# Weight loads in 4 KB rows, column groups for a two-column product, and gathers issued ahead of their stage, in a two-block transformer kernel

## Chip, cores and metric

The kernel runs on one core of one Trainium2 chip. The metric is the device time of one execution in microseconds (us), the median of the runs taken. One launch computes everything.

## What is computed

Two blocks of two layers each (`DEPTH = 2`) over 256 tokens of width 1024, float32 throughout. The second block also carries 256 context tokens of its own.

```python
def first_block(x, ...):
    for l in range(DEPTH):
        h = rms_norm(x, attn_norm_g[l])
        pa, pb, pc = split_sizes(h @ w_in[l], (A_PROJ, B_PROJ, C_PROJ))
        ya = rwkv7_mixer(pa, ...); yb = dilated_mixer(pb, ...); yc = mla_mixer(pc, ...)
        x = x + jnp.concatenate([ya, yb, yc], axis=-1) @ w_out[l]
        h = rms_norm(x, ffn_norm_g[l])
        x = x + (jax.nn.silu(h @ ffn_w_gate[l]) * (h @ ffn_w_up[l])) @ ffn_w_down[l]

def second_block(x, c, ctx, c_ctx, ada_w, ada_b, ...):
    for i in range(DEPTH):
        mod = jax.nn.silu(c) @ ada_w[i] + ada_b[i]          # one row of 6 * 1024
        modc = jax.nn.silu(c_ctx) @ ada_w[i] + ada_b[i]     # and one for the context
        ...                                                 # modulated norms, attention, projection
        x = x + g2 * peer_ffn(h2, ...)
        if not last:
            xc = xc + cg2 * peer_ffn(h2c, ...)

def peer_block(hb, w_q, sub_keys, u_tab, v_tab):
    ...                                    # 8 heads x 16 experts for each token
    u = u_tab[expert]                      # gathered rows of 1024 floats
    act = jax.nn.gelu(jnp.einsum('nhkd,nd->nhk', u, hb))
    w = g * act
    return jnp.einsum('nhk,nhkd->nd', w, v_tab[expert])
```

## The kernel before

The program is a sequence of stages (`stage`, L151). In each the five engines run their own streams, kept in order by semaphores, and each ends in a block end and a barrier (L157 to L161): an engine drains its own work, and all wait for the last. The order is: the modulation of the second block's first layer; qkv, attention and projection of the context tokens; their expert queries (the choice of 128 expert slots per token, `SLOTS`); then the first block, two layers of in_projection, rwkv, latent_heads, first_attention, out_projection and feed_forward; then the second block's latent tokens: qkv, attention, out projection, peer_queries, experts, twice.

**Weights.** `WeightRing` (L164) has three slots in SBUF (`WSLOTS`). A group of weights is one image [128, n] in HBM, mostly n = 4096 floats for 8 k-tiles by 512 columns: 16 KB per partition, 2 MB, loaded by one `dma_start` of SyncE (`load_to`, L175). Before loading over slot g - 3, SyncE waits until `w_used` says that TensorE is through with it. For that TensorE, after the last product of each group, waits for its own product semaphore and then adds one to `w_used` (L411 for the in projection; such a pair stands behind each group in every stage). A layer of the first block has 5 groups for in_projection, 6 of the modulation weights of the second block's second layer (used inside rwkv), 1 for the latent queries, 1 for the latent keys and values, 2 for out_projection, 11 for gate and up, 6 for down.

**Modulation.** [silu(c), silu(c_ctx)] are two columns. For each of 12 groups of 512 output columns (L1499) the stationary operand is silu[:, k, :] (128x2) and the weights [128, 512] move, eight k-tiles into two PSUM partitions; ScalarE copies the two rows out and four transposes (L1509) turn them into columns. In rwkv the same product is done in parts (`mod_part`, L485) between the levels of a triangular inverse, copied by ScalarE to a row buffer and written to HBM (`kept_mod`) by one DMA per group; the second layer's experts stage reads it back and transposes it.

**Context expert rows.** The context tokens' experts are not computed in a stage of their own: `ContextRows` (L1222) spreads 232 gathers per layer of the first block over its stages. A row is one indirect DMA of GpSimd (L1249) that brings one expert's 1024 floats for each of 128 tokens, 4 KB per partition, 512 KB in all, into one of four slots (`CTX_RING`). U rows (slots 0 to 127) are each consumed by one VectorE instruction with a sum (L1261), V rows by one that adds a weighted row to a running sum (L1265). Between them stand the gelu weights (`gelu_weights`), in feed_forward ahead of the first V rows. `SHARE` says how many rows each stage has: in_projection 26, rwkv 70, latent_heads 4, attention 14, out_projection 12, feed_forward 106. `fetch` issues them in the stage that takes them, each waiting until the row four before has been taken; `take(v, n)` stands in VectorE's stream between its other work, three rows per tile in in_projection and feed_forward, and `take_rest` takes what is left at the stage's end. `ContextTail` does the same for 48 last rows in the second block's first layer.

In feed_forward, for each of 22 tiles (`FF_TILES`) TensorE does gate and up (32 products of 256 columns), ScalarE the sigmoid, VectorE the two multiplications (`acted`), with four PSUM banks in turn: TensorE can't start tile j before tile j - 4 is multiplied. Then come the down products, 352 of them.

Of the kernel before, what the change touches and what calls it, by code (L numbers as in the profile page):

```python
# [7 lines left out]
F32 = mybir.dt.float32  # L8
# [44 lines left out]
WSLOT = KT * 544  # L53

# [109 lines left out]
class WeightRing:  # L164
# [10 lines left out]
    def load_to(self, eng, g1):  # L175

        for g in range(self.started, min(g1, len(self.sizes))):
            if g >= WSLOTS:
                eng.wait_ge(self.mem.w_used, g - WSLOTS + 1)
            n, at = self.sizes[g], self.offsets[g]  # L180
            eng.dma_start(self.slot(g)[:, 0:n], self.images[at:at + P * n].rearrange("(p n) -> p n", p=P)
                          ).then_inc(self.mem.w_landed[g % WSLOTS], 16)
        self.started = max(self.started, min(g1, len(self.sizes)))

    def landed(self, eng, g):
        eng.wait_ge(self.mem.w_landed[g % WSLOTS], 16 * (g // WSLOTS + 1))
# [175 lines left out]
def in_projection(nc, m, d, ring, l, rows):  # L362

    with stage(nc, NORM_SEMS + " loras prod_done evacuated mixed step_v h_in",
# [6 lines left out]
        dest = [b.pad[:, j, 1:SEQ + 1] for j in range(A_TILES)]  # L371
# [18 lines left out]
        def _(pe):  # L390
            norm_pe(pe, m, s, b, SEQ)
            for j, (g, c, n) in enumerate(tiles):
# [45 lines left out]
def rwkv(nc, m, d, ring, l, rows):  # L438
# [13 lines left out]
    with stage(nc, sems, bufs) as (block, s, b):  # L452
# [14 lines left out]
        mod_row = lambda n: m.mix[0:2, 2 + 2 * (n % 2):4 + 2 * (n % 2), :].rearrange("p f t -> p (f t)")  # L467

        @block.sync
        def _(sp):  # L470
            for n in range(MODS):
                ring.load_to(sp, g0 + G_MOD + WSLOTS + n + 1)
                sp.wait_ge(s.mod_copied, n + 1)
                sp.dma_start(m.kept_mod[:, 512 * (l * MODS + n):512 * (l * MODS + n + 1)], mod_row(n)).then_inc(
                    mod_kept(n), 16)
            for n in range(2):
                sp.wait_ge(mod_kept(n), 16 * MODS // 2)
# [6 lines left out]
        def _(pe):  # L484
            def mod_part(n, k0, k1):  # L485
# [6 lines left out]
                for k in range(k0, k1):  # L492
                    ins = pe.matmul(m.ps[0:2, mod_bank(n), :], m.silu[:, k, :], w[:, k, :], start=(k == 0),
                                    stop=(k == KT - 1), skip_group_check=True)
                if k1 == KT:
                    ins.then_inc(s.mod_done, 1)
                    pe.wait_ge(s.mod_done, n + 1)
                    pe.sem_inc(m.w_used, 1)
# [16 lines left out]
            mod_part(0, 0, KT)  # L515
# [24 lines left out]
            for lev in range(LEVELS):  # L540
# [12 lines left out]
                mod_part(lev, 0, 2)  # L553
# [7 lines left out]
                mod_part(lev, 2, KT)  # L561
# [1665 lines left out]
```

## Time and profile before

| | us |
|---|---|
| median of 3 runs (3628.1 to 3643.7) | 3635.93 |
| the profiled execution | 3640.52 |
| its span, first to last instruction | 3638.7 |

Over the span TensorE is busy 76%, VectorE 61%, GpSimd 33%, ScalarE 16%, with a mean granted TensorE clock of 0.909. The DMA engines move 1026 MB, 282 GB/s. A shared view of busy times says little here, since the stages have different limits. In the profile's 40 slices the expert stages stand out (DMA 9, some 420 GB/s), and between them stand stretches at 70 GB/s. The stages, from the trace:

| stage | from | to, us |
|---|---|---|
| modulation | 0.8 | 103.8 |
| context qkv, attention, projection, queries | 105 | 365 |
| layer 0: in_projection | 370.4 | 450.6 |
| rwkv | 451.8 | 650.9 |
| latent_heads | 653.5 | 679.8 |
| attention | 681.6 | 727.1 |
| out_projection | 728.2 | 762.3 |
| feed_forward | 762.8 | 1060.4 |
| layer 1, the same six stages | 1062.8 | 1760.5 |
| latent qkv, attention, projection, queries | 1785 | 2032 |
| experts | 2032 | 2697 |
| qkv, attention, projection, queries | 2698 | 2969 |
| experts | 2969 | 3632 |

The names in the rows below: `ps` is PSUM, `w_ring` the weight slots, `ctx_ring` the four row slots, `in_peer_u`, `in_peer_v` the expert tables. SPq, ACTq and POOLq are the queues' issuing instructions; q0 holds the DMA packets of the gathers, q1 those of the weight loads.

### The profile page before, as it was taken

The numbers are of one execution on the slowest core, as the hardware profiler recorded it, in microseconds if no ns is written. First come the engines' busy times: TensorE is split into PE (matmuls) and PEld (weight loads), VectorE is DVE, ScalarE is ACT, GpSimd is POOL, SyncE is SP. The second block draws the span as 40 slices with busy tenths as digits, with TensorE's granted clock in tenths as the row PEclk, the third lists the DMA queues.
The fourth block names the chain that finished last, engine by engine and source line by source line (L and its number), as shares of the span: only waits on it lengthen the run. The fifth ranks groups of instructions, "written<-read, shape, count | busy, mean of one in ns | idle before, by whom it ended". The sixth has DMA issues, their size and how long they took to land. (4 is left out here: it accounts for less than half of the span.)

```text
span 3638.7 us, 31139 instructions
## 1 busy us (share of the span) xinstructions
PE 2775.6 (76%) x10098; PEld 1770.8 (49%) x10098; DVE 2227.2 (61%) x5250; ACT 581.0 (16%) x1595; POOL 1187.8 (33%) x1028
## 2 busy tenths in 40 slices
PE   8893778599937868997489587777779957777776
PEld 1672646478735556786457232232237743233222
DVE  0439576755556757545676787665546377766555
ACT  0311110210002002000131111111112211111111
POOL 0000344234543432445222244444410014444442
PEclk9996988899968969998699799999989989999999
DMA  8322776578868746788455699999961239999997
GB/s 339 129 93 72 266 266 228 168 276 324 325 245 298 276 167 219 296 327 324 150 170 180 267 420 420 421 421 421 420 246 70 71 140 421 420 419 421 421 420 304
DMA packets 166034, 1026.31 MB, mean 282 GB/s; under 512 B 18552, under 2 KB 19544, under 8 KB 86896
## 3 DMA queue, kind: packets, MB, share of 16 engines
q0 software_dynamic: 147456, 805.37, 56.8%
q1 hardware_dynamic: 17552, 214.67, 15.5%
q10 hardware_dynamic: 864, 4.28, 0.3%
q8 instruction: 81, 1.33, 0.1%
q14 instruction: 81, 0.66, 0.1%
HBM read 1020.53 MB, written 3.72 MB: 281 GB/s over the span
## 5 line engine op out<-in xcount | busy, mean ns | idle before, releaser
L2140 PE MATMUL ps<-w_ring,diag 128*128 128x512 f32 x1216 | 577.2, 621 | 173.5 <-ACT diag L2103 173.3
L1249 POOL DMA_INDIRECT ctx_ring<-in_peer_u,ctx_expert x256 | 306.1, 1196 | 871.7 <-POOLq L161 478.2
L2023 DVE SCALAR_TENSOR_TENSOR w_ring<-w_ring,htok 128x1024 f32<-128x1024 f32 x304 | 372.2, 1225 | 237.8 <-DMA w_ring<-in_peer_uv,expert 237.3
L2140 PEld LDWEIGHTS ps<-w_ring,diag 128*128 128x128 f32 x1216 | 227.3, 195 | 519.2 <-ACT diag L2103 279.3
L2140 PE MATMUL ps<-own,diag 128*128 128x512 f32 x624 | 312.5, 643 | 204.1 <-ACT diag L2103 204.1
L2010 POOL DMA_INDIRECT w_ring<-in_peer_uv,expert x304 | 333.4, 1097 | 409.5 <-PE ps L2140 397.4
L1261 DVE SCALAR_TENSOR_TENSOR ctx_ring<-ctx_ring,h_now 128x1024 f32<-128x1024 f32 x256 | 306.7, 1224 | 143.8 <-DMA ctx_ring<-in_peer_u,ctx_expert 135.1
L1249 POOL DMA_INDIRECT ctx_ring<-in_peer_v,ctx_expert x208 | 275.7, 1326 | 297.9 <-DVE sum L1265 120.8
L2010 POOL DMA_INDIRECT own<-in_peer_uv,expert x156 | 164.0, 1051 | 631.3 <-POOLq L161 364.5
L1167 PE MATMUL ps<-mix,w_ring 128*128 128x256 f32 x1408 | 316.8, 387 | 19.0 <-DVE mix L354 8.6
L2140 PEld LDWEIGHTS ps<-own,diag 128*128 128x128 f32 x624 | 117.5, 200 | 392.3 <-ACT diag L2103 277.6
L1167 PEld LDWEIGHTS ps<-mix,w_ring 128*128 128x128 f32 x1408 | 270.9, 194 | 65.0 <-issue 23.8
L2023 DVE SCALAR_TENSOR_TENSOR own<-own,htok 128x1024 f32<-128x1024 f32 x156 | 191.0, 1225 | 136.8 <-DMA own<-in_peer_uv,expert 136.7
L2103 ACT ACTIVATE diag<-consts_sb,w 128x128 f32<-128x128 f32 x512 | 177.5, 394 | 576.5 <-DVE w L2040 576.5
L1265 DVE SCALAR_TENSOR_TENSOR low<-ctx_ring,ctx_weight,low 128x1024 f32<-128x1024 f32 x104 | 133.5, 1283 | 120.5 <-DMA ctx_ring<-in_peer_v,ctx_expert 115.9
L1265 DVE SCALAR_TENSOR_TENSOR sum<-ctx_ring,ctx_weight,sum 128x1024 f32<-128x1024 f32 x104 | 133.5, 1283 | 119.5 <-DMA ctx_ring<-in_peer_v,ctx_expert 114.5
L326 PE MATMUL ps<-sq,consts_sb 128*128 128x256 f32 (+1 forms) x96 | 38.3, 575 | 194.6 <-ACT sq L334 194.6
L1182 PE MATMUL ps<-act,w_ring 128*128 128x256 f32 x704 | 154.8, 380 | 3.7 <-PE ps L1182 2.8
L1182 PEld LDWEIGHTS ps<-act,w_ring 128*128 128x128 f32 x704 | 132.8, 190 | 25.7 <-issue 8.1
L2098 ACT ACTIVATE th<-th 128x2 f32<-128x2 f32 x256 | 52.1, 203 | 525.5 <-DVE th L2032 525.5
L1891 PE MATMUL ps<-hT,w_ring 128*128 128x256 f32 x512 | 121.2, 393 | 9.9 <-issue 5.0
L406 PE MATMUL ps<-mix,w_ring 128*128 128x256 f32 x544 | 122.6, 386 | 7.6 <-DVE mix L354 6.1
(395 smaller groups left out, 4092.2 us busy)
## 6 DMA issues: line engine op xcount, KB each, us to landing
w_ring<-in_weights SPq DMA_DIRECT2D x93, 2048.0 KB, 9.2
w_ring<-in_peer_uv,expert POOLq DMA_INDIRECT x304, 15.8
w_ring<-in_weights SPq DMA_DIRECT2D x2, 2176.0 KB, 10.6
ctx_ring<-in_peer_u,ctx_expert POOLq DMA_INDIRECT x256
w_ring<-in_weights SPq DMA_DIRECT2D x4, 1024.0 KB, 8.0
ctx_ring<-in_peer_v,ctx_expert POOLq DMA_INDIRECT x208
own<-in_peer_uv,expert POOLq DMA_INDIRECT x156, 16.6
consts_sb<-in_consts ACTq DMA_DIRECT2D x1, 1867.0 KB, 17.6
```

The lines of the kernel that those rows point to most:

```text
L406: ins = pe.matmul(m.ps[:, j % BANKS, 0:SEQ], w[:, k, c:c + P], m.hT[:, k, 0:SEQ], start=(k == 0), stop=(k == KT - 1))
L1167: ins = pe.matmul(m.ps[:, GU[j % 4], part * SEQ:(part + 1) * SEQ], w[:, k, (j % 2) * P:(j % 2 + 1) * P], m.hT[:, k, 0:SEQ], start=(k == 0) ...
L1182: ins = pe.matmul(m.ps[:, 2 + o // 2, (o % 2) * SEQ:(o % 2 + 1) * SEQ], w[:, kk, o * P:(o + 1) * P], b.act[:, j, :], start=(j == 0 and o % ...
L1249: pool.indirect_dma_start(out=m.ctx_ring[:, r % CTX_RING, :], out_offset=None, in_=expert_tables(self.d)[r // SLOTS], in_offset=bass.Indir ...
L1261: v.scalar_tensor_tensor(out=row, in0=row, scalar=1.0, in1=m.h_now[:, :], op0=ALU.mult, op1=ALU.mult, accum_out=m.ctx_dots[:, k:k + 1]).th ...
L1265: v.scalar_tensor_tensor(out=m.tail_sum[self.l], in0=row, scalar=m.ctx_weight[:, self.l, k:k + 1], in1=m.tail_sum[self.l], op0=ALU.mult, o ...
L1891: ins = pe.matmul(m.ps[:, j % 4, 0:SEQ], w[:, k, (j % 4) * P:(j % 4 + 1) * P], m.hT[:, k, 0:SEQ], start=(k == 0), stop=(k == KT - 1))
L2010: pool.indirect_dma_start(out=entry(e), out_offset=None, in_=table, in_offset=bass.IndirectOffsetOnAxis(ap=m.expert[:, blk, k:k + 1], axis ...
L2023: v.scalar_tensor_tensor(out=u, in0=u, scalar=1.0, in1=m.htok[:, blk, :], op0=ALU.mult, op1=ALU.mult, accum_out=b.dots[:, e:e + 1]).then_i ...
L2098: act.activation(th, th, ACT.Tanh, scale=math.sqrt(2 / math.pi)).then_inc(s.tanh_out, 1)
L2103: act.activation(b.diag[:, e % DIAGS, :], m.ident, ACT.Copy, scale=b.w[:, e:e + 1]).then_inc(s.built, 1)
L2140: ins = pe.matmul(m.ps[:, 2 * blk + half, :], b.diag[:, e % DIAGS, :], entry(e)[:, D + half * 512:D + (half + 1) * 512], start=(k == 0), s ...
```

## The change

- `load_to` splits each group into pieces of 1024 floats per partition (`PIECE`): four DMAs of 512 KB instead of one of 2 MB, with rows of 4 KB instead of 16 KB. `landed` waits for all of a group's pieces.
- `w_used` is gone. `load_to` gets a function that names, for each group of this stage, the product semaphore and count after which the slot is free; SyncE waits on that. TensorE's wait and increment behind each group go. Groups of earlier stages need no wait, since the barrier has passed.
- The two-column product uses column groups: `silu` gets 32 columns, 30 of them zero, and for each of two steps four matmuls of different k-tiles write four ranges of 32 PSUM partitions. The four partial sums are added afterwards, in modulation by a product with a 128x2 matrix `pick` of ones in place of the transpose, in the experts stage by four accumulating products for each one. In rwkv two steps stand where eight were; `kept_mod` has eight rows, written by four small DMAs per group.
- `fetch` issues the first four rows of the next stage at the end of this one.
- `SHARE`: in_projection 26 to 40, feed_forward 106 to 92. `feed_forward` takes four rows per tile.
- The gelu weights move from feed_forward into the beginning of out_projection (`weigh`), since all U rows are now done by the end of attention.

```diff
+PIECE = 1024
-    def load_to(self, eng, g1):
+    def load_to(self, eng, g1, g0=0, done=None):
         for g in range(self.started, min(g1, len(self.sizes))):
-            if g >= WSLOTS:
-                eng.wait_ge(self.mem.w_used, g - WSLOTS + 1)
+            if done and g - WSLOTS >= g0:
+                eng.wait_ge(*done(g - WSLOTS - g0))
             n, at = self.sizes[g], self.offsets[g]
-            eng.dma_start(self.slot(g)[:, 0:n], self.images[at:at + P * n].rearrange("(p n) -> p n", p=P)
-                          ).then_inc(self.mem.w_landed[g % WSLOTS], 16)
+            image = self.images[at:at + P * n].rearrange("(p n) -> p n", p=P)
+            for c in range(0, n, PIECE):
+                eng.dma_start(self.slot(g)[:, c:min(c + PIECE, n)], image[:, c:min(c + PIECE, n)]
+                              ).then_inc(self.mem.w_landed[g % WSLOTS], 16)
@@ in_projection (and likewise in each stage with weights)
-            ring.load_to(sp, g0 + G_MOD + WSLOTS)
+            ring.load_to(sp, g0 + G_MOD + WSLOTS, g0 + G_IN, lambda n: (s.prod_done, last_tile[n]))
-                if j + 1 == len(tiles) or tiles[j + 1][0] != g:
-                    pe.wait_ge(s.prod_done, j + 1)
-                    pe.sem_inc(m.w_used, 1)
@@ rwkv
-                sp.dma_start(m.kept_mod[:, 512 * (l * MODS + n):512 * (l * MODS + n + 1)], mod_row(n)).then_inc(
-                    mod_kept(n), 16)
+                for q in range(COLUMN_GROUPS):
+                    sp.dma_start(m.kept_mod[2 * q:2 * q + 2, 512 * (l * MODS + n):512 * (l * MODS + n + 1)], mod_row(n)[GROUP * q:GROUP * q + 2, :]).then_inc(
+                        mod_kept(n), 16)
-                mod_part(lev, 0, 2)
+                mod_part(lev, 0, 1)
-                mod_part(lev, 2, KT)
+                mod_part(lev, 1, 2)
@@ out_projection
+            if weigh_rows:
+                rows.weigh(v, chain(v, s.step_w), s, b.th[:, :])
@@ feed_forward
-                if j == U_TILES:
-                    ...
-                rows.take(v, 3 if j >= U_TILES else min(3, SLOTS - rows.taken))
+                rows.take(v, 4)
@@ ContextRows
-    SHARE = dict(in_projection=26, rwkv=70, latent_heads=4, attention=14, out_projection=12, feed_forward=106)
+    SHARE = dict(in_projection=40, rwkv=70, latent_heads=4, attention=14, out_projection=12, feed_forward=92)
     def fetch(self, pool, name):
-        for r in range(first, end):
+        for r in range(first + CTX_RING if first else 0, min(end + CTX_RING, 2 * SLOTS - CTX_TAIL)):
@@ modulation
+def column_group_products(pe, m, bank, w, k0, k1):
+    for k in range(k0, k1):
+        for q in range(COLUMN_GROUPS):
+            ins = pe.matmul(m.ps[GROUP * q:GROUP * (q + 1), bank, :], m.silu[:, 2 * q + k, :], w[:, 2 * q + k, :],
+                            start=(k == 0), stop=(k == 1), skip_group_check=True)
-                    for k in range(KT):
-                        ins = pe.matmul(m.ps[0:2, g % 2, :], m.silu[:, k, :], w[:, k, :], start=(k == 0), stop=(k == KT - 1))
+                    ins = column_group_products(pe, m, g % 2, w, 0, 2)
-                        ins = pe.transpose(m.ps[:, 2, c:c + 2], b.row[:, (g - 1) % 2, j * P:(j + 1) * P], m.ident[0:2, 0:2])
+                        ins = pe.matmul(m.ps[:, 2, c:c + 2], b.row[:, (g - 1) % 2, j * P:(j + 1) * P], b.pick[:, :],
+                                        start=True, stop=True)
```

## Rows read from the trace of the kernel before

**Rows 1.** Windows: us, busy (xcount) of PE, PEld, DVE, ACT, POOL, PEclk, DMA share, GB/s
```profile
0.00:104.00 104.00, 89.83 (x240) 19.30 (x240) 7.46 (x18) 10.88 (x16) 0.20 (x4) 1.00 0.85 330
...
763.00:1062.00 299.00, 236.63 (x1056) 202.28 (x1056) 161.21 (x171) 9.92 (x24) 138.89 (x106) 0.91 0.82 306
2032.00:2714.00 682.00, 500.68 (x1074) 199.95 (x1074) 441.84 (x1281) 124.01 (x407) 277.50 (x256) 0.95 0.98 405
```

**Rows 2.** Timeline of PE in modulation: start, us, engine, line, operation, count [idle before]
```profile
86.29 7.03 PE L1499 MATMUL ps<-w_ring,silu 128*2 128x512 f32 x16
93.47 0.38 PE L1509 MATMUL ps<-consts_sb,row 2*128 2x2 f32 x4
```

**Rows 3.** Windows, columns as in Rows 1, a stretch inside modulation
```profile
4.00:46.00 42.00, 35.29 (x87) 7.15 (x88) 6.85 (x15) 3.84 (x6) 0.00 (x0) 1.00 1.01 421
```

**Rows 4.** Timeline of DVE in the in projection: its first and last row taken
```profile
384.79 1.22 DVE L1261 SCALAR_TENSOR_TENSOR ctx_ring<-ctx_ring,h_now 128x1024 f32<-128x1024 f32 x1
...
449.39 1.23 DVE L1261 SCALAR_TENSOR_TENSOR ctx_ring<-ctx_ring,h_now 128x1024 f32<-128x1024 f32 x1 [6.44 <-DMA ctx_ring<-in_peer_u,ctx_expert]
```

**Rows 5.** Timeline of the feed-forward: products, the last rows, the next stage
```profile
796.84 14.05 PE L1167 MATMUL ps<-mix,w_ring 128*128 128x256 f32 x64 [0.31 <-PE ps L1167]
...
1004.31 7.14 PE L1182 MATMUL ps<-act,w_ring 128*128 128x256 f32 x32 [0.31 <-PE ps L1182]
...
1050.18 1.08 POOL L1249 DMA_INDIRECT ctx_ring<-in_peer_v,ctx_expert  x1 [0.30 <-issue]
...
1055.35 2.67 DVE L1265 SCALAR_TENSOR_TENSOR sum<-ctx_ring,ctx_weight,sum 128x1024 f32<-128x1024 f32 x2 [0.96 <-DMA ctx_ring<-in_peer_v,ctx_expert]
1057.94 2.47 DVE L1217 TENSOR_TENSOR xT<-xT,ps 128x512 f32<-128x512 f32 x4
...
1062.84 0.07 DVE L425 MEMSET pad<- 128x9 f32 x1 [2.42 <-PEq L161]
```

**Rows 6.** DMA of 1022 to 1050 us (first row), then of 799.5 to 805
```profile
DMA packets 2094, 7.60 MB, mean 271 GB/s; under 512 B 239, under 2 KB 239, under 8 KB 2094
...
DMA packets 172, 2.07 MB, mean 376 GB/s; under 512 B 9, under 2 KB 9, under 8 KB 58
...
q0 software_dynamic: 58, 0.20, 10.7%
```

**Rows 7.** DMA of 783 to 925 us: queues (packets, MB, share) and issues
```profile
q0 software_dynamic: 6888, 25.07, 48.0%
q1 hardware_dynamic: 1440, 20.97, 37.8%
...
ctx_ring<-in_peer_v,ctx_expert POOLq DMA_INDIRECT x49
```

**Rows 8.** DMA issues of the page: count, KB each, us to landing
```profile
consts_sb<-in_consts ACTq DMA_DIRECT2D x1, 1867.0 KB, 17.6
```

**Rows 9.** Timelines of DVE and PE in rwkv: row waits, products with the inverse
```profile
458.43 1.23 DVE L1261 SCALAR_TENSOR_TENSOR ctx_ring<-ctx_ring,h_now 128x1024 f32<-128x1024 f32 x1 [4.88 <-DMA ctx_ring<-in_peer_u,ctx_expert]
...
528.54 1.22 DVE L1261 SCALAR_TENSOR_TENSOR ctx_ring<-ctx_ring,h_now 128x1024 f32<-128x1024 f32 x1 [6.75 <-DMA ctx_ring<-in_peer_u,ctx_expert]
...
518.73 2.02 PE L546 MATMUL ps<-inv,ms 128*128 128x128 f32 x16 [0.30 <-PE ps L493]
...
534.77 3.11 PE L546 MATMUL ps<-inv,ms 128*128 128x128 f32 x16 [3.20 <-DVE ms L716]
```

**Rows 10.** Line L157, 636 to 660 us: durations ns min/median/max, first and last start
```profile
L157 POOLq DRAIN  x2: 8637/8782/8927, 639.5 to 655.4; - x2
```

**Rows 11.** Timeline of DVE: last rows taken by latent heads, attention, out projection
```profile
676.00 1.23 DVE L1261 SCALAR_TENSOR_TENSOR ctx_ring<-ctx_ring,h_now 128x1024 f32<-128x1024 f32 x1
...
721.98 1.22 DVE L1261 SCALAR_TENSOR_TENSOR ctx_ring<-ctx_ring,h_now 128x1024 f32<-128x1024 f32 x1
...
752.32 1.23 DVE L1261 SCALAR_TENSOR_TENSOR ctx_ring<-ctx_ring,h_now 128x1024 f32<-128x1024 f32 x1 [7.10 <-DMA ctx_ring<-in_peer_u,ctx_expert]
```

More of the change, by code:

```diff
@@ L370, in in_projection @@
                  (3, 0, 512), (3, 0, 512), (3, 256, 512), (3, 384, 512), (4, 0, 256), (4, 128, 256)]
+        last_tile = [1 + max(j for j, tile in enumerate(tiles) if tile[0] == g) for g in range(G_MOD - G_IN)]
         dest = [b.pad[:, j, 1:SEQ + 1] for j in range(A_TILES)]
@@ L491, in mod_part @@
                 w = view(KT, 512)(ring.slot(g0 + G_MOD + n))
[L492 to L495, printed above, removed]
+                ins = column_group_products(pe, m, mod_bank(n), w, k0, k1)
+                if k1 == 2:
                     ins.then_inc(s.mod_done, 1)
-                    pe.wait_ge(s.mod_done, n + 1)
-                    pe.sem_inc(m.w_used, 1)
             pe.wait_ge(s.acted, 3)
@@ L1059, in _, with out_projection @@
             rows.take_rest(v, "attention")
-def out_projection(nc, m, ring, group, src, dst, gate, rows=None):
-    with stage(nc, "prod_done added squared summed root", [("sq", [P, KT, SEQ], F32)]) as (block, s, b):
+def out_projection(nc, m, ring, group, src, dst, gate, rows=None, weigh_rows=False):
+    with stage(nc, "prod_done added squared summed root step_w tanh_in tanh_out", [("sq", [P, KT, SEQ], F32), ("th", [P, SLOTS], F32)]) as (block, s, b):
         @block.sync
         def _(sp):
-            ring.load_to(sp, group + NG_O + WSLOTS)
+            ring.load_to(sp, group + NG_O + WSLOTS, group, lambda n: (s.prod_done, 4 * (n + 1)))
         if rows:
@@ L1131, in feed_forward @@
 def feed_forward(nc, m, d, ring, l, rows):
-    with stage(nc, NORM_SEMS + " gu_done sig_done gated acted down_done added step_v tables_in step_w tanh_in tanh_out",
-               [("act", [P, FF_TILES, SEQ], F32), ("sg", [P, 4, SEQ], F32), ("th", [P, SLOTS], F32)]) as (block, s, b):
+    with stage(nc, NORM_SEMS + " gu_done sig_done gated acted down_done added step_v tables_in",
+               [("act", [P, FF_TILES, SEQ], F32), ("sg", [P, 4, SEQ], F32)]) as (block, s, b):
         sources = [(m.xT, 0, SEQ)]
@@ L1138, in feed_forward @@
         last = l == DEPTH - 1
-        U_TILES = -(-(SLOTS - rows.until["feed_forward"][0]) // 3)
         GU = (0, 1, 6, 7)
@@ L1237, in __init__ @@
             self.until[name] = (at - n, at)
-        assert self.until["feed_forward"][0] < SLOTS and at == 2 * SLOTS - CTX_TAIL and at % CTX_RING == 0
+        assert self.until["attention"][1] == SLOTS and at == 2 * SLOTS - CTX_TAIL and at % CTX_RING == 0
     def fetch(self, pool, name):
@@ L1296, in fetch @@
         self.end_of_stage = end
-        for t in range(first, end):
+        for t in range(first + CTX_RING if first else 0, min(end + CTX_RING, self.rows)):
             if t >= CTX_RING:
@@ L1353, in first_layer @@
         first_attention(nc, m, d, b2, rows)
[L1354 removed]
+    out_projection(nc, m, ring, FIRST_AT + l * G_FIRST_END + G_OUT, m.mix, m.xT, None, rows, True)
     feed_forward(nc, m, d, ring, l, rows)
@@ L1482, in _ @@
                     act.wait_ge(s.turned, g - 1)
-                act.activation(b.row[:, g % 2, :], m.ps[0:2, g % 2, :], ACT.Copy).then_inc(s.copied, 1)
+                act.activation(b.row[:, g % 2, :], m.ps[:, g % 2, :], ACT.Copy).then_inc(s.copied, 1)
             act.wait_ge(s.reduced, 1)
@@ L1564, in _ @@
         def _(sp):
-            ring.load_to(sp, g0 + NG_QKV + WSLOTS)
+            ring.load_to(sp, g0 + NG_QKV + WSLOTS, g0, lambda n: (s.prod_done, 4 * (n + 1)) if n < 2 else (s.v_done, N // P))
         if rows:
@@ L2121, in turn_context @@
                 for z in range(2):
-                    ins = pe.transpose(m.ps[:, 2, z * 6 * KT:(z + 1) * 6 * KT], products[:, z, :], m.ident[0:6 * KT, 0:6 * KT])
+                    for q in range(COLUMN_GROUPS):
+                        ins = pe.matmul(m.ps[:, 2, z * 6 * KT:(z + 1) * 6 * KT], products[:, 2 * q + z, :],
+                                        m.ident[0:6 * KT, 0:6 * KT], start=(q == 0), stop=(q == COLUMN_GROUPS - 1))
                 ins.then_inc(s.products_turned, 1)
```

85 lines of the change are left out of this document (37 added, 48 removed).

## The prediction

> **What bounds the kernel now.** I read the stages first, then each engine's waits inside a stage, then the transfer queues over short windows. The windows by stage [rows 1] show one kernel with several limits. The two expert stages at the end (682 us the first, the second much alike) move 405 GB/s with the DMA engines 0.98 busy; the change doesn't touch their transfers, so 1,350 us stand still. The first stage, modulation, has TensorE busy 89.8 of 104 us. In its timeline [rows 2] a group is 16 matmul instructions in 7.03 us and four small transposes in 0.38, and the next begins 7.48 after it: TensorE sets the pace, while DMA alone could do 421 GB/s [rows 3], that is 2.097 MB in 5.0 us. In the two layers of the first block VectorE consumes gathered rows of 524 KB through a ring of four, beside the weight loads. The in projection ends on such a row: the last of 26 is waited for 6.44 us and done at 450.6 [rows 4]. The feed-forward is TensorE-bound while it has products (14.05 us for 64 matmuls, 0.31 idle, then the next weight group), but these end at 1004.31 + 7.14 = 1011.45, while rows are fetched and taken until 1058 and the next stage starts at 1062.8: 51 us are a tail of rows [rows 5].
>
> **How fast rows come.** With no weights in flight 7.60 MB land in 28 us [rows 6], 271 GB/s, 1.93 us a row. Beside a weight load of 16 KB packets q0 (rows) gets 0.20 MB of 2.07 MB in 5.5 us [rows 6], 376 in all. Over 142 us of the feed-forward the rows get 25.07 MB and the weights 20.97 MB [rows 7]. If rows run at 271 while weights rest and both together at 376 (the total of the 5.5 us window) while they load, the load is active A us with 0.376A + 0.271(142 - A) = 46.04 MB: A = 72, weights at 291 and rows at 85 GB/s, a fifth: packet against packet, 4 KB against 16. The mean is 142/49 = 2.90 us a row.
>
> **The change part by part.**
> *Weights in 4 KB rows.* Packets become equal, so I take half of 376 for each while a load is active: 11.2 us per 2.097 MB load, in which 4.0 rows land (2.79 us each), and 1.93 outside. No row shows a 4 KB weight stream beside gathers. Bounds: no better than now (2.9), and all at 421 GB/s. SyncE issues four transfers for one; only its own waits stand behind them.
> *Modulation, 12 groups in column groups.* If four matmuls run beside each other the 7.03 us become 1.8; if not they stay. The four products with the picking matrix replace 0.38 us by at most 1.8: 0.44 each, twice what a product with a full 128x128 weight load takes in the feed-forward (0.22). TensorE then needs 3.6 us a group and DMA 5.0: DMA decides. Before the last of the 12 groups lands, 25.2 MB of them and 4.3 MB of tables and inputs (the largest is in [rows 8], 1.9 MB; two more have 1 MB each) pass: 29.4 MB at 421 is 70; with the start I take 74 (an estimate). The last product is at 76 instead of 100.8, the end behind it is 1.4 longer: -23. TensorE will now rest a quarter of the time; where it falls to its lower level (1.2 GHz, the granted clock is 1.00 now [rows 1]) both parts double, 7.2 us a group, no gain. I take -21, with -3 as the near end. The Trainium skill (TensorEngine Tiling (Array Packing), Theoretical Speedup) gives up to 4 times for 32 columns; no row here has two matmuls side by side, so the other end, none, is a rival below.
> *The six modulation groups inside each rwkv stage* lose the same 5 us each, but VectorE sets the level loop: its rows and waits. TensorE waited for it only 3.2 us once, and ran straight on behind its own modulation products once (0.30 idle) [rows 9]. Nothing is gained; with longer rests TensorE's clock may stay low (16 products took 3.11 after such a rest against 2.02), cover for which is the row wait.
> *In projection, 40 rows for 26.* It now has 36 rows after the first four, and five loads of 9.44 MB: 50 us active at 2.79, 18.0 rows, the other 18.0 at 1.93: 85 us, 2.36 us a row. The fifth lands at 391 (issued with the first take at 384.8 [rows 4]; from issue at 1050.2 to use at 1055.4 is 5.2 us [rows 5]), the last at 391 + 85 = 476 less half a row that the five loads leave free, 474; its take ends at 475 against 450.6: +24.
> *Gathers four ahead.* Before each stage end Pool issues the next stage's four rows, released by the last takes, and must then drain. Where gathers are in flight its drains take long, 8.6 and 8.9 us [rows 10], about what a gather takes to land, and every engine waits in the barrier for it. So a stage now ends no earlier than its last take, plus up to 1 us until Pool issues the last row for the slot, plus 5.2 to land: about 6 later. That costs +6 at the in projection and +6 at rwkv, whose last takes are the stage's last work; latent heads' last take ends at 677.2, the stage at 680: +2.7; attention's at 723.2, the stage at 727: +1.5; in the out projection the 7.1 us of waiting become less, but its last take stays near the end: +2.3 [rows 11]. The gain: 4.88 us of waiting at rwkv's start go, and of the 6.75 us wait in the level loop I take 2.6, the row that comes sooner [rows 9]; elsewhere the first rows were in time. In the latent block the takes end 6 to 9 us ahead of the stage: 0.
> *Feed-forward, 92 rows for 106, four per tile.* Two tiles now want 8 rows and a load: 11.2 us for 4.0 rows and 7.7 for the others, 18.9 us against TensorE's 14.36. So products are held back by `acted`: rows 5 to 72 (67 at 2.36 = 158 us) from 782.8 put tile 18's activation at 943; the last tiles' products end at 950, half a group later, and then come the down products (352 at 0.22 us, 77.4), which end at 1028, adds 2.5, barrier 2.4: 1032 to 1033 against 1062.8, -30. No tail of rows is left; what is late next is TensorE, throttled.
> *Gelu weights in the out projection.* Six VectorE steps, a tanh and the memset, some 5 us, now stand at a stage start where TensorE has 128 products of 0.22 us (28 us) ahead of it and VectorE 12 rows and 8 adds (under 20): hidden; without that cover 5 us per layer.
> *Slots freed by product semaphores.* TensorE no longer waits for its own products: 0.31 us per weight group [rows 5]. Some 40 groups lie where TensorE sets the pace, half of them behind another wait: -6. SyncE's waits name other semaphores, with nothing else queued behind.
>
> **The sum**, against the profiled execution (3638.7 span, 3640.5 with what lies around it, 4.6 above the median 3635.9): -21 modulation; per layer +24 +6 (in projection), -7.5 +6 (rwkv), +2.7, +1.5, +2.3, -30, together +5, twice +10; -6. That is -17: 3623.5 for that execution, **3619** for the median.
>
> **The rivals.**
> *Rows gain more (B).* If rows and weights move at 421 together, a row costs 2.0 to 2.1: in projection +12, feed-forward at TensorE's own end (1008), -55. Layer -31; sum -21 -62 -6, -89: 3547. For it: 421 is reached in modulation and by the expert rows. Against: with four rows in the ring even an idle DMA gives 271.
> *Rows gain nothing (C), the slower side.* Place: in projection and gate/up products. Each 1 us on a row costs 35 in the one and 67 in the other, twice: 204. From 2.44 us the kernel is slower than before (17/204 above 2.36); at 2.75 to 2.9 it is +65 to +75, 3705. For it: 8 rows and a load are 6.3 MB, in 14.36 us 439 GB/s, over anything in the trace; the ring of four already lets DMA idle. Against: equal packets.
> *Column groups don't overlap, or small transfers are slow (D).* 7.03 stays and 1.8 is added to 0.38: 12 x 1.4 = +17 in place of -21, +38 on the forecast: 3657. The same result comes if 512 KB pieces move as the 512 KB gathers do, 271 GB/s: 29.4 MB then take 108 us. The Trainium skill (DMA: Bandwidth & Descriptors, Measured) wants at least 1 MiB a transfer for three quarters of the peak, which speaks for this; several pieces in flight speak against.
> *Pool's drain doesn't hold the stage (E).* Then the +18.5 per layer go: 3582.
>
> **How the numbers follow.** Forecast (3619, from 3595 to 3645) 0.46, B 0.19, C 0.17, D 0.09, E 0.09. This measurement can tell 0.5%, 18 us, from no change. Faster: half of the forecast's case less a little (0.23), B, E's 0.09: 0.51. Same: 0.21 of the forecast's, 0.05 of D: 0.26. Slower: 0.02, C's 0.17, 0.04 of D: 0.23. The range leaves out a tenth at either end, most of C's far end and a little of B: 3550 to 3690.
>
> **What would show it.** Modulation's groups 5 us apart with TensorE waiting for w_ring, its stage near 83 us; row landings 2.3 to 2.4 us apart in the in projection and the feed-forward, q0 and q1 near equal beside a load; the in projection 110 us long, ended by rows and a Pool drain; TensorE in gate/up products idle behind `act`, the last row taken long before the last product. Wrong if rows stay 2.8 apart, if TensorE's 16 instructions of a modulation group still take 7 us, or if stages end before the prefetched rows land.

## The result, and the profile after

The changed kernel takes 3681.9 us (median of 4 runs, 3675.4 to 3688.1) against 3638.0 for the kernel before beside it: 1.2% slower, ratio 1.0121 with a 95% interval of 1.0095 to 1.0146. It is inside the outer range that the prediction gave (3550 to 3690), outside the range of its forecast (3595 to 3645), and slower than the kernel before, where the forecast of 3619 was faster. The profiled execution has a span of 3681.7 against 3638.7, at a mean granted clock of 0.880 against 0.909.

The stages of the two traces, each from its first instruction to the first of the next, tell where the 43 us come from (us; two values are the two layers). Three borders lie later than that: modulation, the second feed_forward and the first experts stage are counted up to the first product with weights of the stage behind them, so they hold its norm too, and modulation begins at 0.8 us. Up to the barrier modulation goes from 105.1 to 85.7 us and the second feed_forward from 300.3 to 270.6.

| stage | before | after | difference | forecast |
|---|---|---|---|---|
| modulation | 113.7 | 94.9 | -18.8 | -21 |
| in_projection | 81.4, 84.9 | 116.5, 112.6 | +35.1, +27.7 | +30 each |
| rwkv | 201.8, 204.9 | 212.6, 211.5 | +10.8, +6.6 | -1.5 each |
| latent_heads | 28.1, 28.1 | 33.5, 33.1 | +5.4, +5.0 | +2.7 each |
| attention | 46.5, 46.7 | 49.2, 48.1 | +2.7, +1.4 | +1.5 each |
| out_projection | 34.9, 34.8 | 42.7, 43.7 | +7.8, +8.9 | +2.3 each |
| feed_forward | 299.7, 323.7 | 264.0, 293.1 | -35.7, -30.6 | -30 each |
| latent stages with gathers (four) | 246.8 | 256.6 | +9.8 | 0 |
| all others | 1857.8 | 1864.4 | +6.6 | -6 (the semaphores) |

Windows by stage of the changed kernel, columns as in [rows 1], which they answer: modulation, in projection, rwkv and feed-forward of layer 0.

```profile
0.00:84.00 84.00, 49.42 (x288) 19.92 (x288) 8.21 (x22) 11.00 (x16) 0.20 (x4) 0.82 0.99 393
351.70:468.00 116.30, 74.63 (x320) 64.27 (x320) 61.02 (x108) 11.62 (x29) 51.51 (x44) 0.81 0.80 289
468.00:681.00 213.00, 129.12 (x725) 108.06 (x725) 141.24 (x212) 25.99 (x39) 90.99 (x70) 0.70 0.64 219
...
806.00:1070.00 264.00, 239.48 (x1056) 206.63 (x1056) 141.61 (x149) 9.73 (x23) 101.77 (x88) 0.96 0.82 301
```

Modulation has changed its bound: the DMA engines are 0.99 busy at 393 GB/s, and TensorE 49 of 84 us, where it was 90 of 104. Its timeline, against [rows 2]:

```profile
66.72 3.62 PE L1461 MATMUL ps<-w_ring,silu 128*32 128x512 f32 x16 [2.21 <-DMA w_ring<-in_weights]
70.28 1.05 PE L1513 MATMUL ps<-pick,row 128*128 128x2 f32 x8
71.84 1.92 PE L1461 MATMUL ps<-w_ring,silu 128*32 128x512 f32 x16 [0.51 <-DMA w_ring<-in_weights]
```

The 16 products of a group take 1.92 us where they took 7.03, and 3.62 in a stretch at a granted clock of 0.54 (66.7 to 70.4 us; 1.00 from 71.8 to 73.8): four of them do run beside each other. TensorE now waits for `w_ring`. The two next groups are 5.1 us apart.

The in projection ends on a gap that was not there. DVE's timeline at its end, the last row and the next stage's first work, against [rows 4], whose last row had 1.2 us to the next stage:

```profile
457.50 1.23 DVE L1247 SCALAR_TENSOR_TENSOR ctx_ring<-ctx_ring,h_now 128x1024 f32<-128x1024 f32 x1
...
468.28 0.74 DVE L668 TENSOR_SCALAR kk<-low,vectors 128x256 f32<-128x256 f32 x2 [9.54 <-PEq L162]
```

9.5 us pass, and the line that GpSimd spends them in is the drain (line L158, 455 to 470 us; durations in ns, then start), against [rows 10]:

```profile
L158 DVEq DRAIN  x1: 1265/1265/1265, 457.5 to 457.5; - x1
L158 POOLq DRAIN  x1: 8357/8357/8357, 458.8 to 458.8; - x1
```

VectorE's own drain takes 1.3 us, GpSimd's 8.4. The last packet of the gathers ends at 464.9, 2.2 us before that drain does.

In the feed-forward the tail of rows [rows 5] is gone: the last row is taken 237 us into the stage and the down products end at 260. But the groups of the two pages differ in what TensorE waits for; the changed kernel's row:

```profile
L1165 PE MATMUL ps<-mix,w_ring 128*128 128x256 f32 x1408 | 330.3, 399 | 60.3 <-DVE act L1198 38.5
```

TensorE is idle 60.3 us ahead of its gate and up products (19.0 before), 38.5 of them for `act`, VectorE's multiplication, which stands in line behind four rows per tile.

Beside a weight load the two queues now share evenly (DMA of 415 to 421 us), against [rows 6]:

```profile
q1 hardware_dynamic: 340, 1.25, 52.0%
q0 software_dynamic: 315, 1.17, 48.8%
```

The gathers have 48% of the bytes (1.17 of 2.41 MB), where they had 10%.

### The profile page after: what moved, and what is told of

It is laid out like the page before. It is cut to its first block and busy times, and to the rows that moved or that the text cites. A ratio compares the mean times of both kernels' runs of the same rounds, so it can differ in the third digit from the quotient of the medians.

```text
span 3681.7 us, 31502 instructions
## 1 busy us (share of the span) xinstructions
PE 2723.8 (74%) x10160; PEld 1811.3 (49%) x10160; DVE 2230.9 (61%) x5254; ACT 581.7 (16%) x1595; POOL 1176.4 (32%) x1028
## 5 line engine op out<-in xcount | busy, mean ns | idle before, releaser
L1235 POOL DMA_INDIRECT ctx_ring<-in_peer_u,ctx_expert x256 | 316.2, 1235 | 857.6 <-DVE ctx_ring L1247 428.0
L2145 PE MATMUL ps<-own,diag 128*128 128x512 f32 x624 | 322.1, 660 | 203.2 <-ACT diag L2106 203.0
L1165 PE MATMUL ps<-mix,w_ring 128*128 128x256 f32 x1408 | 330.3, 399 | 60.3 <-DVE act L1198 38.5
L1235 POOL DMA_INDIRECT ctx_ring<-in_peer_v,ctx_expert x208 | 246.4, 1184 | 329.2 <-DVE sum L1251 146.5
L1165 PEld LDWEIGHTS ps<-mix,w_ring 128*128 128x128 f32 x1408 | 281.3, 201 | 109.5 <-issue 38.1
L1897 PE MATMUL ps<-hT,w_ring 128*128 128x256 f32 x512 | 120.6, 392 | 16.7 <-DVE hT L357 16.7
L413 PE MATMUL ps<-mix,w_ring 128*128 128x256 f32 x544 | 120.9, 385 | 6.4 <-DVE mix L360 6.4
L1295 POOL DMA_INDIRECT tail_ring<-in_peer_v,ctx_expert x48 | 53.1, 1107 | 200.0 <-DVE sum L1308 90.1
```

The source lines that it names most:

```text
L413: ins = pe.matmul(m.ps[:, j % BANKS, 0:SEQ], w[:, k, c:c + P], m.hT[:, k, 0:SEQ], start=(k == 0), stop=(k == KT - 1))
L1165: ins = pe.matmul(m.ps[:, GU[j % 4], part * SEQ:(part + 1) * SEQ], w[:, k, (j % 2) * P:(j % 2 + 1) * P], m.hT[:, k, 0:SEQ], start=(k == 0) ...
L1235: pool.indirect_dma_start(out=m.ctx_ring[:, r % CTX_RING, :], out_offset=None, in_=expert_tables(self.d)[r // SLOTS], in_offset=bass.Indir ...
L1295: pool.indirect_dma_start(out=m.tail_ring[:, t % CTX_RING, :], out_offset=None, in_=expert_tables(self.d)[1], in_offset=bass.IndirectOffse ...
L1897: ins = pe.matmul(m.ps[:, j % 4, 0:SEQ], w[:, k, (j % 4) * P:(j % 4 + 1) * P], m.hT[:, k, 0:SEQ], start=(k == 0), stop=(k == KT - 1))
L2145: ins = pe.matmul(m.ps[:, 2 * blk + half, :], b.diag[:, e % DIAGS, :], entry(e)[:, D + half * 512:D + (half + 1) * 512], start=(k == 0), s ...
```

## The experiments

The changes were taken apart first from the one end and then from the other. Seven of the kernels make a ladder in which each step is one part:

| kernel | us | step |
|---|---|---|
| before | 3638 | |
| x11: product semaphores | 3621 | -17 |
| x10: and column groups in modulation | 3611 | -10 |
| x8: and 4 KB rows | 3589 | -22 |
| x6: and column groups in rwkv | 3596 | +8, within what the runs of each vary |
| x1: and 40 / 92 rows, four per tile, gelu weights moved | 3614 | +18 |
| after: and four gathers ahead | 3682 | +68 |

**x1, without the gathers ahead**

```diff
-        for r in range(first + CTX_RING if first else 0, min(end + CTX_RING, 2 * SLOTS - CTX_TAIL)):
+        for r in range(first, end):
```

> The changed kernel with one part undone: each stage's first four gathers are issued in that stage again, not at the end of the one before. Theory 1 (the gathers ahead hold the stage ends: GpSimd's drain waits for them): the stage ends lose what they gained in the change, 8.3 us at the in projection, 9.3 at rwkv, 5.4 at latent heads, 2.6 at attention, 7.7 at the out projection, in two layers, and 11 in the latent block, 77 in all; the first rows of a stage come later again, 5 us at rwkv's start and a few elsewhere, some 8 per layer: 3682 - 77 + 16 = 3621. Rival (the rows themselves are the limit, wherever they are issued): each stage starts later by what it ends sooner, no change, 3682.

Measured: 3614.0 us, ratio to before 0.9950 (0.9932 to 0.9968). The gathers ahead are worth 68 us, and what is left of the change is faster than the kernel before. The stages show it: in_projection 107.6 and 108.6, rwkv 200.2 and 204.0, latent_heads 27.6 and 27.5, out_projection 36.3 and 36.2.

**x2, 16 KB rows in the changed kernel, and x4, 4 KB rows alone in the kernel before** (the diff is x2's)

```diff
-PIECE = 1024
+PIECE = WSLOT
```

> The changed kernel with one part undone: each weight group is one load with rows of 16 KB again, instead of four pieces of 4 KB rows. Theory 2 (packet sizes share the DMA engines: beside a load the gathers got 84 to 98 GB/s with 16 KB rows and 160 to 173 with 4 KB rows): a row costs 2.9 to 3.0 us instead of 2.5, on 36 rows in the in projection and 67 in the feed-forward, twice: 3682 + 206 x 0.45 = 3775. Rival (rows are bound by the ring of four, not by the share): within 10 us of 3682. Modulation: the same 83 us if 2 MB loads and 512 KB pieces are equal there.

> The kernel before with one part of the change: weight loads in four pieces with rows of 4 KB. Theory 2 (packet sizes share the DMA engines): a row costs 2.5 us instead of 2.95, so the in projection's 22 waited rows save 10 us, and the feed-forward's tail of 51 us shrinks by 100 rows x 0.45 = 45, in both layers: 3638 - 110 = 3528. Rival (small transfers cost as much as they give, or rows are bound by their ring): 3638 within 15.

Measured: x2 3718.1 us (1.0238, 1.0211 to 1.0264), 36 over the changed kernel; x4 3617.1, 20 under the kernel before (0.9951, 0.9932 to 0.9970). The sign is theory 2's, the size two fifths of it in x2 (36 of 93) and a fifth in x4 (20 of 110). A row of the feed-forward costs, from the first taken to the last, 2.67 us before, 2.48 in x4, 2.44 after and 2.57 to 2.60 in x2. The DMA view of x4 over the 142 us of its feed-forward that answer [rows 7], both windows beginning 19.9 us into the stage (792.3 to 934.3 us, since x4's stage begins at 772.4):

```profile
q0 software_dynamic: 7929, 28.87, 53.5%
q1 hardware_dynamic: 5751, 20.94, 40.8%
```

The gathers' share during a load went from 10 to 48%, and over the stretch they move 28.9 MB instead of 25.1, 15% more, beside the same 21 MB of weights. The total rose from 46.1 to 49.9 MB, 325 to 351 GB/s. Both feed-forwards of x4 are shorter by it, 20.7 and 22.1 us, where theory 2 had 45 each; the in projections gain 0.8 and 4.7, where it had 10 each. Modulation is slower than before, 120.6 against 113.7 us, for which no run isolates a cause. (The profiled x4 is its fastest run, 12 to 15 us under the others.) In x2 16 of the 25 us between the two profiled runs lie in the feed-forwards, 6 in the in projections and 14 in the latent_heads and out_projection stages, where the last gather has to land beside a weight load; the other stages give some back.

**x3 and x8, the product inside rwkv in eight two-column products again**

```diff
-                ins = column_group_products(pe, m, mod_bank(n), w, k0, k1)
-                if k1 == 2:
+                for k in range(k0, k1):
+                    ins = pe.matmul(m.ps[0:2, mod_bank(n), :], m.silu[:, k, 0:2], w[:, k, :], start=(k == 0),
+                                    stop=(k == KT - 1), skip_group_check=True)
+                if k1 == KT:
```

> The changed kernel with column groups kept in modulation, but the modulation product inside rwkv done in eight two-column products again (and its results stored as two rows, read back with two transposes). Theory 3 (inside rwkv those long products were what kept TensorE's granted clock up, 0.80 before, 0.70 now, and the level loop waits for TensorE at the lower clock): rwkv gets 6 us shorter per layer, from first row taken to last, granted clock back near 0.80, and the experts stage loses its pause of some 4 us: 3682 - 16 = 3666. Rival (VectorE and rows set rwkv, TensorE's clock is covered): 3682, and only the clock moves.

> The kernel of the run with the shares of before and no gathers ahead (label x6), with the modulation product inside rwkv in eight two-column products again. Theory 3 (column groups there let TensorE's granted clock fall, and the level loop waits for it): rwkv 3 us shorter per layer, the experts stage 3: 9 less than that run. Rival: within 4 us of it.

Measured: x3 3682.7 (1.0135, 1.0114 to 1.0156) against 3681.9 for the changed kernel; x8 3588.9 (3583 to 3595) against 3596.5 for x6 (3590 to 3599). The windows of rwkv in the first layer, of x3 and then of x8:

```profile
468.90:678.10 209.20, 146.75 (x724) 102.55 (x725) 140.71 (x212) 25.89 (x38) 92.78 (x70) 0.79 0.65 223
```

```profile
433.70:641.20 207.50, 148.83 (x724) 102.28 (x724) 140.92 (x212) 25.88 (x38) 90.76 (x70) 0.78 0.67 232
```

The granted clock comes back, from 0.70 to 0.79 and 0.78 (x6 has 0.74), and the stage doesn't follow: 209.2 against 212.6 in x3, but 207.5 against 202.5 in x8 (in the second layer 208.4 against 211.5, and 206.1 against 208.0). Theory 3 falls as a cause of the result; a few us either way stay open, as the two pairs disagree.

**x5, four gathers ahead alone in the kernel before**

> The kernel before with one part of the change: the first four gathers of a stage are issued at the end of the stage before. Theory 1 (GpSimd's drain holds every stage end until the last gather has landed): the same price as in the changed kernel, where it was 68 us by time: 3638 + 68 = 3706, with some 8 us from last row taken to next stage at the in projection, where it is 1.2 now. Rival (the price hangs on the changed shares, whose in projection ends on rows with nothing else left, while with 26 rows its products end with the rows): +35 to +45, 3678.

Measured: 3725.0 us, ratio 1.0237 (1.0215 to 1.0259), 85 us more than before. So the price doesn't hang on the changed shares. In_projection is 92.3 us twice, out_projection 44.1 and 46.2, latent_heads 37.1 and 34.1; its last in-projection row is taken 73.8 us into the stage, sooner than before, and the stage ends 11 us later. The expectation had 8 us from the last row taken to the next stage, and it is 18.5 here (11.0 in layer 1):

```profile
444.90 0.94 POOL L1249 DMA_INDIRECT ctx_ring<-in_peer_u,ctx_expert  x1 [0.30 <-issue]
...
462.29 0.74 DVE L667 TENSOR_SCALAR kk<-low,vectors 128x256 f32<-128x256 f32 x2 [18.50 <-PEq L161]
```

The last gather ahead is issued at 444.9 beside a weight load of 16 KB rows, and its last packet ends at 459.4. That fits a price of 85 us here and 68 in the changed kernel with its 4 KB rows.

**x6, the shares of before, and x7, three rows per tile** (both without gathers ahead)

```diff
-    SHARE = dict(in_projection=40, rwkv=70, latent_heads=4, attention=14, out_projection=12, feed_forward=92)
+    SHARE = dict(in_projection=26, rwkv=70, latent_heads=4, attention=14, out_projection=12, feed_forward=106)
```

```diff
-                rows.take(v, 4)
+                rows.take(v, 3)
```

> The changed kernel without gathers ahead, and with the shares of before (in projection 26 rows, feed-forward 106, three rows per tile, gelu weights in the feed-forward). Theory 4 (14 rows moved ahead cost 27 us in the in projection, and give 10 to 16 in the feed-forward, where four rows per tile hold TensorE's products back): 3614 - 2 x 27 + 26 = 3586. Rival (rows are a fixed stream, it is indifferent which stage has them): 3614 within 8.

> The changed kernel without gathers ahead, with its own shares (40 and 92 rows), but three rows per tile taken in the feed-forward in place of four. Theory 5 (with four per tile VectorE's row waits hold back the gate and up products, which now end 184 to 190 us into the stage and not 163 to 169): products end 241 us into the stage, the last row at 12.6 + 92 x 2.48 = 241 too, the stage is 247 long and not 269 and 261: 3614 - 36 = 3578. Rival (the rows' stream sets the stage in either order, since 8 rows and a weight load need 18 us): 3614 within 8.

Measured: x6 3596.5 (0.9884, 0.9866 to 0.9901) and x7 3582.5 (0.9844, 0.9818 to 0.9870), against 3614.0 for x1. Taking three rows per tile is worth 32 us, and with it 40 and 92 rows are no worse than 26 and 106. The reason is in one row of x7's groups of instructions (781 to 945 us, all the gate and up products of layer 0):

```profile
L1165 PE MATMUL ps<-mix,w_ring 128*128 128x256 f32 x704 | 155.2, 384 | 4.4 <-DVE mix L360 4.4
```

No wait for `act` is left. The down products begin 158 us into the stage, not 189, and the rows left over are taken beside them: rows end at 252 and products at 234, where x1 had rows at 242 and products at 265 (all counted from the stage's start). The stage is 255.4 us long against 269.1.

**x9 and x13, two and three gathers ahead in the changed kernel**

```diff
-        for r in range(first + CTX_RING if first else 0, min(end + CTX_RING, 2 * SLOTS - CTX_TAIL)):
+        for r in range(first + 2 if first else 0, min(end + 2, 2 * SLOTS - CTX_TAIL)):
```

> The changed kernel with the gathers issued ahead of a stage cut from four to two. Theory 1 (each stage end waits for the landing of the last gather issued, however many there are): the price stays, 3682 within 12. Rival (the price goes with the rows in flight at the stage end): half of the 68 us goes, 3648.

> The changed kernel with three gathers issued ahead of a stage in place of four (none gave 3614, two 3626, four 3682). Theory 7 (a stage ends when the last gather issued in it has landed and GpSimd's drain is through; the last one of n rows ahead can be issued only when the row four before it is taken, so with four it is the stage's last take that releases it, and each row less lets it go one take, 1.3 to 2.6 us, sooner, until it is hidden behind the last takes): between the two, 3640 to 3660. Rival (what costs is that all four slots are in flight at the barrier, three or fewer are nearly free): within 8 of 3626.

Measured: x9 3625.8 (0.9960, 0.9944 to 0.9977), x13 3642.6 (1.0006, 0.9990 to 1.0023). With none, two, three and four ahead the time is 3614, 3626, 3643 and 3682: theory 1 in its first form (the number doesn't matter) and its rival (half of the price goes) both missed x9, theory 7 foretold x13 before it ran, its rival did not. A ring of more than four slots, which would part the number ahead from the row that releases it, was not run. One boundary in three kernels, rwkv to latent_heads of layer 0, shows how: GpSimd's last issue, VectorE's last row, the next stage's first work on ScalarE. With none ahead (x1):

```profile
646.72 1.68 POOL L1235 DMA_INDIRECT ctx_ring<-in_peer_u,ctx_expert  x1 [0.73 <-DVE ctx_ring L1247]
...
656.35 1.22 DVE L1247 SCALAR_TENSOR_TENSOR ctx_ring<-ctx_ring,h_now 128x1024 f32<-128x1024 f32 x1
...
660.28 0.63 ACT L965 ACTIVATE csq<-low 128x512 f32<-128x512 f32 x1 [12.24 <-PEq L162]
```

With two (x9):

```profile
657.15 0.94 POOL L1235 DMA_INDIRECT ctx_ring<-in_peer_u,ctx_expert  x1 [0.30 <-issue]
...
663.57 1.22 DVE L1247 SCALAR_TENSOR_TENSOR ctx_ring<-ctx_ring,h_now 128x1024 f32<-128x1024 f32 x1
...
668.41 0.63 ACT L965 ACTIVATE csq<-low 128x512 f32<-128x512 f32 x1 [13.55 <-PEq L162]
```

With four (the changed kernel), and GpSimd's drain:

```profile
670.00 0.95 POOL L1235 DMA_INDIRECT ctx_ring<-in_peer_u,ctx_expert  x1 [0.30 <-issue]
...
667.67 1.22 DVE L1247 SCALAR_TENSOR_TENSOR ctx_ring<-ctx_ring,h_now 128x1024 f32<-128x1024 f32 x1
...
680.88 0.63 ACT L965 ACTIVATE csq<-low 128x512 f32<-128x512 f32 x1 [21.69 <-PEq L162]
```

```profile
L158 POOLq DRAIN  x1: 9271/9271/9271, 668.9 to 668.9; - x1
```

From the end of the last row to the next stage: 660.3 - 657.6 = 2.7, 668.4 - 664.8 = 3.6 and 680.9 - 668.9 = 12.0 us. From the last issue's beginning to the next stage: 13.6, 11.3 and 10.9. The second count is nearly fixed for two and four. With none the rows are what is late, and the drain, begun at 646.5, is over before them. With two, the last issue lies 7.6 us ahead of the end of the last row, and its landing is nearly covered. With four, it is the stage's last row that frees the slot; GpSimd, at work on the issue before until 669.7, begins the last one at 670.0, and nothing covers the 5.3 us until landing and the 2.9 that the drain ends behind that.

How long the drain goes on behind the last gather is not fixed. In every stage end with gathers of all the traces it ends behind the last gather packet, and in the first block and the latent stages the distance follows the number of gathers that GpSimd issued in the stage, hardly the kernel:

| gathers issued in the stage | 4 | 12 | 26 | 40 to 44 | 70 | 86 to 92 | 102 to 106 |
|---|---|---|---|---|---|---|---|
| last packet to end of drain, us | 0.5 to 0.8 | 0.8 to 1.1 | 1.5 to 1.6 | 2.0 to 2.2 | 3.2 to 3.3 | 3.9 to 4.3 | 4.5 to 5.8 |

The experts stages, with 256, have 2.4, so the count alone isn't the rule; no run isolates what is. It makes an uncovered gather dearest at the end of a stage with many of them, as rwkv is.

**x10 and x11, the semaphores alone, and with column groups in modulation**

```diff
-                if j % 2:
-                    pe.wait_ge(s.gu_done, j + 1)
-                    pe.sem_inc(m.w_used, 1)
```

> The kernel before with two parts of the change: column groups in modulation alone (rwkv keeps its eight two-column products), and the weight slots freed by product semaphores. Loads are 16 KB rows, shares and gathers as before. From the sum of my parts: modulation 19 us less, the semaphores' 0 to 6: 3638 - 22 = 3616. It is the kernel of label x8 without its 4 KB rows, so theory 2 at the size seen so far (20 us) gives 3589 + 20 to 27 = 3612; a rival, that the two parts work on the same wait, gives under 3600.

> The kernel before with one part of the change: TensorE's wait for its own products and its increment behind each weight group are gone, SyncE waits on the product semaphores. Theory 6: the 0.31 us per group is worth 6 us where TensorE sets the pace: 3632. Rival: it is covered everywhere by rows: 3638 within 3; or the loads start later and it costs: 3644.

Measured: x11 3621.1 (0.9955, 0.9939 to 0.9971), x10 3611.1 (0.9923, 0.9903 to 0.9944). The semaphores are worth 17 us, three times the forecast. In the trace the feed-forwards are 2.9 and 5.5 us shorter (products of the first end at 240.9 and not 248.4), the second in projection 3.0, the rest is spread. Modulation is 92.8 us in x10 against 112.8 in x11; of those 20 us 10 reach the median, and the rest is lost in the first feed-forward of the profiled x10 (305.1 against 296.8), for which I have no cause.

**x12 and x14, put together from the runs**

```diff
-CTX_TAIL = 24
+CTX_TAIL = 28
-    SHARE = dict(in_projection=40, rwkv=70, latent_heads=4, attention=14, out_projection=12, feed_forward=92)
+    SHARE = dict(in_projection=40, rwkv=70, latent_heads=4, attention=14, out_projection=12, feed_forward=88)
-    SHARE = dict(project_qkv=12, attention=14, out_projection=12, peer_queries=10)
+    SHARE = dict(project_qkv=14, attention=16, out_projection=14, peer_queries=12)
```

> A kernel put together from the runs: the changed kernel without gathers ahead, three rows per tile in the feed-forward, eight two-column products inside rwkv, and four rows per layer moved from the feed-forward (88 in place of 92) to the latent stages (56 in place of 48, two more in each of the four), where the DMA engines move 40 to 70 GB/s. If a row is worth its 2.5 us in the feed-forward and costs 1.3 us of VectorE in the latent stages: 3582 - 3 - 20 + 10 = 3569. If the feed-forward then ends on TensorE (its products end 234 us in, the last row 252 and 243): only half of it comes, 3577. If the latent stages end on rows as well, 3585.

> The fastest kernel so far (label x12) with two gathers issued ahead of each stage. Theory 7: the price and the gain nearly cancel, as in the changed kernel, where two ahead cost 12 us against none: 3571 + 12 = 3583. Rival (with rows no longer ending each stage, the earlier first rows give a net gain): 3565.

Measured: x12 3571.1 us (3569.5 to 3573.1), ratio 0.9818 (0.9803 to 0.9833), 2 from what was expected and the fastest of all: 67 us under the kernel before and 111 under the changed one. One number of the expectation is wrong: the four latent stages of the kernel before move 160, 145, 258 and 91 GB/s, not 40 to 70. x14 3580.6 (0.9833, 0.9807 to 0.9858): two gathers ahead cost 10 us here too. The windows of x12 (modulation, in projection, rwkv, feed-forward):

```profile
0.75:93.70 92.95, 52.43 (x304) 23.09 (x304) 11.18 (x27) 15.32 (x26) 0.00 (x0) 0.89 0.97 385
349.40:457.00 107.60, 74.74 (x320) 64.30 (x320) 61.13 (x108) 11.63 (x29) 44.44 (x40) 0.83 0.80 293
457.00:662.00 205.00, 147.66 (x724) 102.87 (x724) 141.05 (x212) 25.92 (x38) 90.67 (x70) 0.77 0.67 227
775.60:1021.00 245.40, 229.83 (x1056) 201.78 (x1056) 136.06 (x145) 9.69 (x23) 107.50 (x88) 0.97 0.91 335
```

Its feed-forward moves 335 GB/s, where the kernel before moved 306 [rows 1], with the products ending 232 us in and the rows 242.

## Why the forecast missed

*Modulation* was right in mechanism and size: four products beside each other, DMA the new bound, -18.8 for -21. The rule that I weighed as a rival, at least 1 MiB a transfer for three quarters of the peak (the Trainium skill, DMA: Bandwidth & Descriptors, Measured), does not hold back the 512 KB pieces here: with several in flight modulation moves 403 GB/s from 4 to 46 us, against 420 with 2 MB loads (x10), and its 93 us in x10 are only 1 to 3 less than with pieces (x9, x1). The other, up to four times for 32 columns (the Trainium skill, TensorEngine Tiling (Array Packing), Theoretical Speedup), agrees: 7.03 / 1.92 = 3.7.

*In projection and feed-forward* came out as the steps said: a row at 2.26 and 2.44 us where 2.36 was worked out, +35 and +28 for +30, -36 and -31 for -30, TensorE idle behind `act`. Without the gathers ahead (x1) the in projections have +26 and +24 for the +24 that the rows were to cost. The step that was passed over is the comparison within the change: four per tile was costed as it stood, and not what three would give, 32 us better.

*4 KB rows*: equal shares beside a load were foreseen and are there, but the whole sum was built on 2.9 us a row for before, from a stretch of 142 us with a load in flight half of the time, where the stage as a whole has 2.67. The part alone is worth 20 us, 36 in the changed kernel; I had put 1 us on a row at 204 us, which would make 0.5 us worth 100. By the same 204, rival C at 2.9 us a row is +93 and not the +75 of its sum.

*Gathers ahead* is the step that failed and that turned the sign. The mechanism was named (the drain waits for the landing; rival E, that it doesn't hold the stage, is out), and its place; price and gain were both mis-sized. It was charged +18.5 and credited -7.5 per layer, 22 us in all, and it measured 68. Three parts of it were wrong.

First, the price of a boundary. A landing of 5.2 us plus up to 1 was counted, 6, and it measured 8.3 and 7.6 at the in projection and 9.3 and 8.8 at rwkv, because the drain goes on behind the landing. This stood in the trace of before: the drain of 639.5 us [rows 10] takes 8.9 us, to 648.5, but the last gather's packets end at 645.2. The prediction read all of the 8.9 as about what a gather takes to land.

Second, the other stages. In the out projection and latent_heads a weight load is in flight at the end: the last gather of the out projection is issued at 796.3 and the next stage starts at 806.2, 10 us later, for +7.8 instead of +2.3 (1.4 of it is there without gathers ahead too, x1). The latent stages were put at nothing, because their rows were read as ending 6 to 9 us ahead of the stage. In the trace of before they end 1.9 us ahead of it in qkv and 3.9 in the out projection, and these two grew by 6.4 and 4.3 us; in attention, where it is 6.9, nothing was added. There too the last taken row releases the last issue.

Third, the credit. rwkv's first row is taken 1.8 us into the stage and not 6.7, as forecast, but its last one is at 200.6 where it was 199.1 (199.6 and 201.8 in layer 1), and 7.5 sooner was forecast. Single profiles vary by more than this: over the eight rwkv stages with four gathers ahead (x2, x3, x5, after) the last row is taken at 195.0 to 200.6, 197.7 in the mean, over the 18 of the nine kernels with none at 197.5 to 205.3, 201.7 in the mean. So some 4 of the 7.5 us are there, about the sooner first row, and of the further 2.6 nothing shows.

*The semaphores* were under-sized, 17 us for 6, and the experts stages were 6.6 us longer with the rest, without a cause that a run isolates (the first of them varies between 681 and 690 in these kernels).

The sum of the misses, 20 us in rwkv (6 of price, 14 of credit), 12 in the out projections, 10 in the latent stages, 13 in the rest and 5 elsewhere, is the distance from -17 to +43. Of the rivals none was the right one: C, rows that gain too little, put the slower side in the rows' rate, and it lies in the stage ends.

## What to carry to other kernels

An operation issued ahead across a barrier is free only if it has landed when the last other work ends: count back from the barrier by issue, landing and drain, and ask what releases its buffer; with a ring of n slots the n-th row ahead is released by the very last consumer, so here the fourth was never covered. An in-order engine that feeds another should do its side work in portions that leave the other fed (three rows per tile, the rest behind the products), even if that leaves a tail. A faster product in a stage bound by another engine moves the clock and not the time.

## What the runs showed of the hardware

GpSimd's drain ends only after its indirect DMAs have landed, 1.8 us (467.1 against 465.3) and 2.9 us (678.2 against 675.3) behind the last landing in the changed kernel; counted from the last packet it is 0.5 us after a stage with 4 gathers and 3.2 after one with 70. Two queues with 4 KB packets share the DMA engines evenly (52% and 49% of the time), while 16 KB packets against 4 KB gave 88% and 11% (from 799.5 to 805 us of the kernel before); over 142 us of the feed-forward the total of both went from 46.1 to 49.9 MB with 4 KB rows alone (x4), and all of the gain is the gathers'. Loads in pieces of 512 KB run at 403 GB/s in modulation where 2 MB loads run at 420 (x10).
